# Requests for expert weights in the order of use: this expert's second matrix, then the next expert's first matrix

## What is computed

```python
def swiglu_clamped(hh):
    x_glu = jnp.minimum(hh[..., ::2], SWIGLU_LIMIT)
    x_lin = jnp.clip(hh[..., 1::2], -SWIGLU_LIMIT, SWIGLU_LIMIT)
    return x_glu * jax.nn.sigmoid(SWIGLU_ALPHA * x_glu) * (x_lin + 1.0)

def moe_ffn(u, w_router, b_router, w1, b1, w2, b2):
    logits = (u @ w_router + b_router).astype(jnp.float32)
    top_vals, top_idx = lax.top_k(logits, TOP_K)
    top_w = jax.nn.softmax(top_vals, axis=-1).astype(u.dtype)
    ...
    def body(acc, inp):
        tok, wt, e = inp
        hb = swiglu_clamped(u[tok] @ w1[e] + b1[e])
        yb = (hb @ w2[e] + b2[e]) * wt[:, None]
        return acc.at[tok].add(yb), None
```

## Time and profile before

| | us |
|---|---|
| median of 3 runs | 1416.4 |
| lowest and highest of the 3 | 1415.99, 1416.95 |
| the profiled execution's own time | 1421.5 |
| its span | 1419.3 |

### The profile page before, as it was taken

One profiled execution on the slowest core, in us unless ns is written; L12 is line 12 of the kernel. 1 busy time (PEld: TensorE's weight loads), 2 busy tenths in 40 slices (PEclk: granted clock), 3 DMA queues, 4 the chain that ended last, 5 costly groups with the idle time before them and its releaser, 6 DMA issues.

```text
span 1419.3 us, 18777 instructions
## 1 busy us (share of the span) xinstructions
PE 1315.8 (93%) x7431; PEld 677.6 (48%) x7431; DVE 391.7 (28%) x942; ACT 272.3 (19%) x629; POOL 44.0 (3%) x48
## 2 busy tenths in 40 slices
PE   9999999799999999998899989998899988999897
PEld 5677787455887534343333433333333333333332
DVE  1055466578213432121111211112111121112112
ACT  2124333456200311111111111111111111111111
POOL 3000100031000000000000000000000000000000
PEclk8999999899999999999999999999999999999999
DMA  9533433234875599999999999999999999999993
GB/s 324 155 120 107 131 122 127 104 113 129 285 252 222 208 412 429 429 429 429 429 429 429 429 429 429 429 429 429 429 429 429 429 429 429 429 429 429 429 375 161
DMA packets 73870, 468.49 MB, mean 330 GB/s; under 512 B 4867, under 2 KB 37915, under 8 KB 49228
## 3 DMA queue, kind: packets, MB, share of 16 engines
q1 hardware_dynamic: 70444, 457.89, 79.6%
q0 software_dynamic: 1952, 5.61, 1.4%
q10 hardware_dynamic: 1440, 4.52, 0.9%
HBM read 466.61 MB, written 1.13 MB: 330 GB/s over the span
## 4 chain that ended last, share of the span: by engine, by line
PE 51%; DMA 44%; ACT 2%; DVE 2%; issue 1%; POOL 0%; SPq 0%; DVEq 0%; ACTq 0%; POOLq 0%
PE bank L1271 49%; DMA ring<-in_w 43%; PE bank L1312 0%; DMA rows<-in_g_ssm 0%; PE bank L1381 0%; DVE ring L970 0%; ACT arena L728 0%; ACT arena L642 0%; PE bank L1556 0%; DVE arena L1104 0%; PE bank L1383 0%; PE bank L1665 0%; DVE arena L933 0%; ACT wdt L811 0%; PE bank L1450 0%
## 5 line engine op out<-in xcount | busy, mean ns | idle before, releaser
L1271 PE MATMUL bank<-ring,arena 128*64 128x512 f32 (+3 forms) x2296 | 577.1, 611 | 76.3 <-DMA ring<-in_w 70.3
L1271 PEld LDWEIGHTS bank<-ring,arena 128*64 128x64 f32 (+2 forms) x2296 | 202.4, 146 | 406.6 <-issue 338.7
L1271 PE MATMUL bank<-arena 128*128 128x64 bf16 (+7 forms) x3048 | 358.2, 356 | 7.8 <-ACT arena L709 4.7
L1271 PEld LDWEIGHTS bank<-arena 128*128 128x128 bf16 (+4 forms) x3048 | 177.1, 121 | 210.4 <-issue 195.4
L1271 PE MATMUL bank<-arena,ring 128*128 128x256 f32 (+2 forms) x1312 | 270.0, 386 | 2.5 <-ACT decays L634 1.6
L1271 PEld LDWEIGHTS bank<-arena,ring 128*128 128x128 f32 (+1 forms) x1312 | 217.4, 181 | 45.3 <-ACT decays L634 1.8
L1185 DVE TENSOR_SCALAR arena<-bank 128x256 f32<-128x256 f32 x64 | 27.1, 423 | 697.4 <-PE bank L1271 697.4
L816 ACT ACTIVATE arena<-arena 128x256 f32<-128x256 f32 x64 | 26.7, 417 | 395.1 <-DVE arena L1185 395.1
L823 ACT ACTIVATE arena<-bank 128x512 f32<-128x512 f32 x32 | 19.1, 597 | 310.4 <-PE bank L1271 310.4
L1271 PE MATMUL bank<-arena,wdt 64*128 64x512 f32 (+1 forms) x280 | 69.4, 602 | 0.7 <-ACT arena L823 0.7
L816 ACT ACT_TABLE_LOAD x32 | 41.1, 1283 | 0.6
(11 more groups left out here) (235 smaller groups left out, 584.6 us busy)
## 6 DMA issues: line engine op xcount, KB each, us to landing
ring<-in_w SPq DMA_DIRECT2D x128, 2048.0 KB, 25.4
arena<-in_w SPq DMA_DIRECT2D x64, 2048.0 KB, 29.2
ring<-in_w_in SPq DMA_DIRECT2D x34, 1024.0 KB, 5.4
ring<-in_w_ssm SPq DMA_DIRECT2D x8, 1024.0 KB, 7.9
arena<-cum_rows ACTq DMA_DIRECT2D x8, 512.0 KB, 4.3
ring<-in_w_att SPq DMA_DIRECT2D x16, 256.0 KB, 6.9
ring<-in_w_out SPq DMA_DIRECT2D x4, 1024.0 KB, 4.8
arena<-bias_rows POOLq DMA_DIRECT2D x1, 2048.0 KB, 11.1
```

What stands on the lines that cost most here:

```text
L1271: return tn.matmul(o, lhsT, rhs, start=first, stop=last, skip_group_check=True)
```

## The change

After `first_experts` step t asks first for the second matrix of expert t + 1, and only then for the first matrix of expert t + 2. The waits keep their counts. `last_two` goes, since in the new order the last experts need no order of their own: the loop over pairs runs 15 times instead of 14, and the last expert's second matrix follows it. The same is done in the loop for overflowing tokens, which is not run. Every request, its size, its source and its buffer stay; no instruction of the four computing engines changes.

```diff
             def step(e, odd, used):
 
-                sources, following = expert_sources(e), expert_sources(e, 1)
-                doubled(following, 1 - odd, used)
-                single(sources, odd, used)
-
-            def last_two(used):
-
-                single(expert_sources(E - 2), 0, used)
-                sources = expert_sources(E - 1)
-                doubled(sources, 1, used)
-                single(sources, 1, used + PARTS)
+                single(expert_sources(e), odd, used)
+                doubled(expert_sources(e, 1), 1 - odd, used)
 
             first_experts()
             PAIR = 2 * PARTS
-            with sp.Fori(0, E // 2 - 2) as pair:
+            with sp.Fori(0, E // 2 - 1) as pair:
                 step(pair * 2 + 1, 1, pair * PAIR)
                 step(pair * 2 + 2, 0, pair * PAIR + PARTS)
-            step(E - 3, 1, (E - 4) * PARTS)
-            last_two((E - 3) * PARTS)
+            single(expert_sources(E - 1), 1, (E - 2) * PARTS)
             sp.wait_ge(flag_ready, 1)
```

More of the change, by code:

```diff
@@ L485, in _ @@
                     doubled(expert_sources(0), 0, b * (E * PARTS) + (E - 2) * PARTS)
-                    with sp.Fori(0, E // 2 - 2) as pair:
+                    with sp.Fori(0, E // 2 - 1) as pair:
                         step(pair * 2, 0, b * (E * PARTS) + (pair * PAIR + (E - 1) * PARTS))
                         step(pair * 2 + 1, 1, b * (E * PARTS) + (pair * PAIR + E * PARTS))
-                    step(E - 4, 0, b * (E * PARTS) + (2 * E - 5) * PARTS)
-                    step(E - 3, 1, b * (E * PARTS) + (2 * E - 4) * PARTS)
-                    last_two(b * (E * PARTS) + (2 * E - 3) * PARTS)
+                    step(E - 2, 0, b * (E * PARTS) + (2 * E - 3) * PARTS)
+                    single(expert_sources(E - 1), 1, b * (E * PARTS) + (2 * E - 2) * PARTS)
                 sp.wait_ge(slot_used, PASSES * E * PARTS - PARTS + 1)
```

## The result

The changed kernel takes 1426.55 us (median of 4 runs, 1425.2 to 1429.16) against 1416.2 for the kernel before (4 runs, 1415.23 to 1416.95): a ratio of 1.007, with a 95% interval of 1.0056 to 1.0084. It is slower by 0.7%, where 0.5% was forecast. The direction and the mechanism of the stage were right, but the median lies 0.55 us above the upper end of the range, 1426.0. Its profiled execution took 1425.2 us with a span of 1423.2.

The account below looks back on a forecast made before the run. The prediction took the stream of 182 transfers at 4.894 us each to bound the stage: 18.65 + 0 + 34.26 - 45.3 + 0 = +7.6 us on 1416.4 gives 1424.0 us, 0.5% slower, range 1421.5 to 1426.0 us.

Parts of the forecast that it names:

- the mechanism of the stage: In the expert stage, the transfer stream sets the pace: later start +18.65 us, later last wait +34.26, less work behind -45.3.

Follow-up runs that it names:

- third trace: The kernel before, run once more unchanged against itself and traced a third time: 1417.17 us (11 runs), ratio 1.0004; span 1413.8 us.
- bridged_early: Against the kernel before: its order kept until a switch at expert 23, one free part asked for ahead there, order of use afterwards; 1407.28 us, ratio 0.9924.

## What to carry to other kernels

Where a stage is bound by one stream of transfers, an order of requests is judged by three things: when its first request can go out, whether the queue ever runs dry, and how much work is left behind the transfer that is waited for last. Asking in the order of use is good for the third and was bad for the first, because the next request in that order had the one buffer that wasn't free, and a wait in the program of the engine that issues the requests holds back those behind it whose buffers are free. So ask in the order in which buffers come free until the consumer has caught up with the stream, put one free part ahead at the switch, and go over to the order of use for the end: 1407.3 us against 1416.9 for before and 1426.4 for the change. And measure such a change from an event that both kernels share, since here the spans of one kernel differ by up to 5.5 us and the lengths of the stage by 0.3. That measures the stage, though, and not the time: the medians moved by 1.6 us more.

## What the runs showed of the hardware

The sum of TensorE's waits hardly moved (70.3 to 73.2 us) while the longest went from 2.3 to 1.3 us, and with that the clock of the stage rose from 0.97 to 1.00. That gained nothing, since the half clock before lay ahead of another wait, at 1347.29 too: there the next second matrix starts 27.60 us later with the half clock and 27.53 us in the third trace without it. A wait of some 2.3 us isn't always followed by half clock: the 16 matmuls behind one of 2.26 us at 1341.85 in the third trace took 3.65 us, as at full clock. Ahead of the stage the clock fell in some executions and not in others, 10 us of it in the first 30 us and a shorter spell at 173 us, for some 4 and 1.7 us of time. The lag of a landing isn't one number: beside the 4.894 us of its bytes it is 2.7 to 3.0 us for the first transfer into an empty queue, and 4.0 to 4.5 hundreds of microseconds later, in a queue that is never empty (the traces of before, of the changed kernel and of bridged_early). And the rate of the stream from 560 to 1340 us is 427 to 428 GB/s in every order tried.
